# Third mixer's inverse in 32x32 and 64x64 blocks at its two last levels; end of the down projection by token groups

## The chip, the cores and the metric

The kernel runs on one core of a Trainium2 chip (trn2). The metric is the device time of one execution in microseconds (us), the median of several runs. The core has TensorE (matmuls, written PE in the profile; PEld are its weight loads), VectorE (DVE), ScalarE (ACT), GpSimd (POOL) and SyncE (SP, which issues transfers here).

## The reference, cut to what matters

One inference step of a decoder layer for 1072 tokens: 16 learned tokens, 1024 prompt tokens, and 8 sequences of 4 tokens. All is fp32.

```python
z = rms(x) @ w_in                         # 1024 -> 7704 columns: four mixers and gates
# mixer 1 HGRN2, mixer 2 RWKV-7, mixer 3 GLA, mixer 4 mLSTM, 4 heads each
# RWKV-7, per token and head (64 x 64 state S):
#   S = S * w_t - (S @ kk_t) outer (kk_t * a_t) + v_t outer k_t ;  y_t = S @ r_t
mix = sum(proj(o_n, w_branch[n]) * sigmoid(gate_n) for n in 4 mixers) @ w_out
x = x + mix
x = x + square(relu(rms(x) @ w_up)) @ w_down      # 1024 -> 4096 -> 1024
y = x * rsqrt(mean(x * x) + 1e-6) * norm_final
```

The RWKV recurrence is evaluated 128 tokens at a time. Within such a tile the tokens depend on each other through a strictly triangular 128 by 128 matrix per head, and the tile's outputs need the inverse of the unit triangular matrix made from it.

## The kernel before, in words

Tokens lie along the free dimension of the tiles, channels along the 128 partitions. The 1056 tokens that have an output (all but the 16 learned ones) are cut into three groups of 352 for every large matmul (`part2(g)`). The large products are made of three fp32r matmuls each: high part times high part, high times low, low times high. The high part is a rounding copy (ScalarE `ACT.Copy`, or VectorE), the low part the difference (`split_lo`, L602). The mixers run in the order mLSTM, then HGRN2 and GLA together, then RWKV-7, which is the third stage of mixer work and is called the third mixer here.

**The third mixer's tiles.** There are eight tiles of 128 tokens (`rw_tile`) and a last one of 48. A tile holds its four heads side by side. TensorE first makes the products of the tile: for each head three fp32 matmuls over the head's 64 channels (L1302 to L1304). Heads 0 and 2 lie on partitions 0 to 63, heads 1 and 3 on 64 to 127. VectorE masks them (L2437, L2458, L2463). Then the inverse is built by doubling: block size 1, 2, 4, 8, 16, 32, 64. At level `l`, with half-size `lh`, TensorE multiplies the off-diagonal matrix with half of the columns of the inverse so far (L1316), ScalarE copies the product to SBUF (L1765), TensorE multiplies from the other side (L1337, and L1331 for the transposed inverse at level 5), and VectorE puts the needed entries in place with a predicated copy (`select`, L2482). For levels 1 to 4 VectorE gets the transposed inverse by a stream transpose (L2447). All these matmuls use the full 128 by 128 matrices, though at the last levels only blocks of 32 by 32 or 64 by 64 are kept by the masks. An fp32 matmul is two records in the profile.

The order on each engine is written out by hand, and engines meet in semaphores. While TensorE would wait for ScalarE or VectorE it does steps of other work: `steps(gate, k)` issues k steps of the gates' input projection (`fill_work`; a step is the three matmuls of L463, 352 columns each). ScalarE takes each finished filler result out of PSUM (L498) between its own steps. On VectorE an increment of the semaphore `select_turn` stands before each predicated copy.

**The end.** The down projection runs in four passes `jj` of two output rows (a row is 128 channels) each: for each of the 32 rows `r` of the hidden layer, ScalarE makes the high part (L1864), VectorE the low part (L602) into two alternating buffers, and TensorE does, for both output rows `v`, the three groups and three products (L1464, 18 matmuls). Every fourth row VectorE also splits a chunk of weights (L598, L602). The passes are a hardware loop. In the last pass, ScalarE squares the first six rows of x (L568), and GpSimd adds the squares up (L575). After the pass, VectorE adds the residual for the rows 6 and 7 (L2672), they are squared and added one after the other, all 1056 tokens wide; TensorE sums over partitions with a matrix of ones (L561, fp32), ScalarE makes the scale with Ln and Exp (L589, L591), and the eight output rows are multiplied, five on VectorE (L2695) and three on GpSimd (L990; ScalarE has multiplied those by norm_final before). SyncE sends each row when it is done (L728), in 8 transfers.

## Time and profile before

| | us |
|---|---|
| median of 3 runs | 2201.63 (2198.26 to 2205.15) |
| profiled execution, its own time | 2207.53 |
| its span, first to last instruction | 2205.9 |
| TensorE busy | 2126.6 |
| VectorE busy | 1038.6 |
| ScalarE busy | 610.8 |
| GpSimd busy | 452.0 |

Times in the profile count from the start of the span. A busy TensorE isn't one at its peak: the ends of its matmuls are modelled and overlap, so how far apart matmuls start says more than their durations. The granted clock is given as a share: 1.00 is 2.4 GHz, 0.50 is 1.2 GHz.

### The profile page before, as it was taken

To read this page: it belongs to the slowest core of one execution; us is meant where nothing else is said; L and a number is where in the kernel's file an instruction comes from. 1 tells how busy PE (TensorE), PEld (TensorE's weight loads), DVE (VectorE), ACT (ScalarE), POOL (GpSimd) and SP (SyncE) were. 2 spreads that over 40 slices of the span, in tenths; PEclk is the share of its full clock that TensorE was granted. 3 is DMA by queue.
4 is the path that set the end of the run, shared out by engine and by line. 5 is a ranking of instruction groups with operands and counts; after the bars stand their busy time and mean duration, and the time that the engine had idled before them with its cause. 6 is when DMAs were issued, how large, how long until landed. Compare 5 with 4: busy or idle time off the path is not lost.

```text
span 2205.9 us, 32891 instructions
## 1 busy us (share of the span) xinstructions
PE 2126.6 (96%) x13203; PEld 2020.8 (92%) x13203; DVE 1038.6 (47%) x1538; ACT 610.8 (28%) x808; POOL 452.0 (20%) x463
## 2 busy tenths in 40 slices
PE   6999999999999989999999999999999999999995
PEld 4998889999999878989899999999999999999994
DVE  4052333566655454343443786522222245665654
ACT  4432224332323163221221541100000023333352
POOL 1122113343544411100001672200000010000022
PEclk9999999999999989999999999999999999999997
DMA  4122125221222322111012762221111251111112
GB/s 163 48 51 83 58 88 167 76 63 63 82 63 86 120 89 69 31 38 39 19 39 98 264 206 88 98 67 48 47 39 67 92 203 55 48 38 48 47 39 88
DMA packets 48705, 177.29 MB, mean 80 GB/s; under 512 B 6416, under 2 KB 6896, under 8 KB 48384
## 3 DMA queue, kind: packets, MB, share of 16 engines
q1 hardware_dynamic: 23184, 85.65, 12.4%
q0 software_dynamic: 17648, 61.31, 8.1%
q10 hardware_dynamic: 7808, 29.41, 3.6%
q8 instruction: 47, 0.77, 0.2%
q14 instruction: 18, 0.15, 0.0%
HBM read 128.84 MB, written 47.51 MB: 80 GB/s over the span
## 4 chain that ended last, share of the span: by engine, by line
PE 85%; DVE 6%; DMA 4%; issue 2%; ACT 2%; POOL 1%; DVEq 0%; SPq 0%; ACTq 0%; POOLq 0%
PE PS L463 27%; PE PS L624 21%; PE PS L1464 16%; PE PS L1337 2%; PE PS L1148 2%; PE PS L1316 2%; PE PS L1426 1%; DMA RING<-in_w_br 1%; PE PS L1160 1%; DVE AR L2135 1%; DMA AR<-proj 1%; PE PS L1009 1%; PE PS L1278 1%; PE PS L1286 1%; DVE CF_parts L598 1%
## 5 line engine op out<-in xcount | busy, mean ns | idle before, releaser
L463 PE MATMUL PS<-HT_parts,WHIA_parts 128*128 128x352 f32 (+1 forms) x1440 | 511.1, 355 | 11.4 <-ACT AR L498 4.1
L463 PE MATMUL PS<-OT_parts,WHIA_parts 128*128 128x352 f32 (+1 forms) x1440 | 474.9, 330 | 0.0
L463 PE MATMUL PS<-HT_parts,RING_parts 128*128 128x352 f32 (+1 forms) x1440 | 473.9, 329 | 0.0
L458 POOL TENSOR_TENSOR RING_parts<-RING,WHIA_parts 128x1024 fp32r<-128x1024 f32 x60 | 151.1, 2519 | 750.3 <-ACT WHIA_parts L453 750.3
L463 PEld LDWEIGHTS PS<-HT_parts,WHIA_parts 128*128 128x128 f32 x1440 | 277.6, 193 | 25.8 <-issue 12.7
L463 PEld LDWEIGHTS PS<-OT_parts,WHIA_parts 128*128 128x128 f32 x1440 | 277.3, 193 | 3.6
L463 PEld LDWEIGHTS PS<-HT_parts,RING_parts 128*128 128x128 f32 x1440 | 276.7, 192 | 0.0
L1464 PE MATMUL PS<-MIXHI_parts,CF_parts 128*128 128x352 f32 x768 | 250.5, 326 | 4.0 <-DVEq L2674 3.0
L624 PE MATMUL PS<-HT_parts,CF_parts 128*128 128x352 f32 x768 | 249.7, 325 | 0.9 <-ACT AR L591 0.9
L1464 PE MATMUL PS<-MIXHI_parts,RING_parts 128*128 128x352 f32 x768 | 249.6, 325 | 0.0
L624 PE MATMUL PS<-HT_parts,RING_parts 128*128 128x352 f32 x768 | 248.4, 323 | 0.0
L624 PE MATMUL PS<-OT_parts,CF_parts 128*128 128x352 f32 x768 | 248.4, 323 | 0.0
L1864 ACT ACTIVATE MIXHI_parts<-AR 128x1056 fp32r<-128x1056 f32 x96 | 104.3, 1087 | 170.1 <-PE PS L1464 164.5
L1464 PEld LDWEIGHTS PS<-MIXHI_parts,CF_parts 128*128 128x128 f32 x768 | 145.1, 189 | 5.9 <-DVEq L2674 3.8
L624 PEld LDWEIGHTS PS<-HT_parts,CF_parts 128*128 128x128 f32 x768 | 144.4, 188 | 1.3 <-ACT AR L591 1.2
L624 PEld LDWEIGHTS PS<-OT_parts,CF_parts 128*128 128x128 f32 x768 | 145.1, 189 | 0.1
L1464 PEld LDWEIGHTS PS<-MIXHI_parts,RING_parts 128*128 128x128 f32 x768 | 144.8, 188 | 0.0
L624 PEld LDWEIGHTS PS<-HT_parts,RING_parts 128*128 128x128 f32 x768 | 144.6, 188 | 0.0
L2634 DVE SCALAR_TENSOR_TENSOR AR<-PS,AR 128x1056 f32 (+1 forms) x32 | 40.2, 1258 | 199.9 <-PE PS L624 193.5
L1464 PE MATMUL PS<-LO_parts,CF_parts 128*128 128x352 f32 x384 | 124.8, 325 | 0.0
L1464 PE MATMUL PS<-CF_parts 128*128 128x352 f32 x384 | 124.6, 324 | 0.0
L575 POOL TENSOR_TENSOR AR<-AR 128x1056 f32<-128x1056 f32 x14 | 33.4, 2385 | 435.6 <-ACT AR L568 435.6
(399 smaller groups left out, 3533.0 us busy)
## 6 DMA issues: line engine op xcount, KB each, us to landing
RING<-in_w_all SPq DMA_DIRECT2D x132, 512.0 KB, 3.3
AR<-gates POOLq DMA_DIRECT2D x32, 528.0 KB, 4.0
proj<-AR ACTq DMA_DIRECT2D x18, 537.0 KB, 5.0
AR<-proj POOLq DMA_DIRECT2D x18, 537.0 KB, 7.3
gates<-CF ACTq DMA_DIRECT2D x16, 528.0 KB, 5.0
gates<-AR ACTq DMA_DIRECT2D x16, 528.0 KB, 5.4
AR<-in_xT SPq DMA_DIRECT2D x8, 537.0 KB, 8.6
AR<-in_xT POOLq DMA_DIRECT2D x8, 528.0 KB, 6.9
```

The costliest lines, as they stand in the source:

```text
L458: e.tensor_tensor(RING_R[:, u], RING[:, u], WHIA_R[:, u].bitcast(F32), ALU.subtract).then_inc(S(f"split{u}"), 1)
L463: last = e.matmul(out, a_[:, u, k, :], b_[:, k, t], start=first and i == 0, stop=end and i == 2)
L575: e.tensor_tensor(sq[:, 0, T2], sq[:, 0, T2], sq[:, 1, T2], ALU.add).then_inc(S("norm_sum"), 1)
L598: return e.tensor_copy(hi, x)
L624: last = e.matmul(PS(3 * u + g, 0, G2), a_[:, u, k, :], b_[:, k, t], start=k == 0 and i == 0, stop=k == KD - 1 and i == 2)
L1009: last = e.matmul(PS(3 + g, 0, GRP)[0:68], WS[:, k, :], XT[:, k, g * GRP:(g + 1) * GRP], start=k == 0, stop=k == KD - 1)
L1148: last = e.matmul(PS(3 * (l % 2), lo * m, hi * m)[0:w], x[:, g, l, 0:w], GQB[:, l % 2, lo * m:hi * m], start=True, stop=True)
L1316: last = e.matmul(PS(4, h * m, h * m + m)[0:w], pb[0:w, 2 * h * w:2 * h * w + w], side, start=True, stop=True)
L1337: last = e.matmul(PS(0, h * m, h * m + m)[0:w], a_[0:w, h * w:h * w + w], b_, start=True, stop=True)
L1464: last = e.matmul(PS(3 * v + g, 0, G2), a_[:, u, 4 * v + r % 4, :], b_[b][:, t], start=r == 0 and i == 0, stop=r == 31 and i == 2)
L1864: e.activation(AHI_R[r % 2][:, T2], act_row(r)[:, T2], ACT.Copy).then_inc(S("act_hi"), 1)
L2634: e.scalar_tensor_tensor(row2(dst), cols2(3 * u), 0.0, row2(RST2), ALU.max, ALU.mult).then_inc(S(f"banks_free{u}"), 1)
```

## The change

Part 1, third mixer, on TensorE alone. The products at a tile's start are issued so that the two partition halves alternate (all nine tiles). At levels 5 and 6 (`lh` 32 and 64) of the eight full tiles, the matmuls are done for the kept blocks only: for each head, two blocks of 32 by 32, or one of 64 by 64, with 32 or 64 partitions contracted. The block lists hold 8 matmuls at level 5 and 4 at level 6, for each group. Two increments of `select_turn` are added on TensorE in each of these levels.

Part 2, the end. The last pass of the down projection is written out behind a loop of three. Its rows 28 to 31 get high and low buffers of their own, and their matmuls are ordered by token group: group 0 for both output rows, then group 1, then group 2. Residual, square, sum, scale and output of each group of 352 tokens follow on their engines, interleaved. GpSimd adds the squares by groups (for the last row of group 2, TensorE adds the square in a second matmul), VectorE makes all output rows, and SyncE sends pairs of rows by group, 12 transfers.

```diff
+        SQ4 = Arena(3 * W).take(t=W)
+        LAST_ROWS = 28
+        LAST_HI = {28: MIXHI_R[:, 0], 29: MIXHI_R[:, 2], 30: MIXHI_R[:, 4], 31: AHI_R[0]}
+        LAST_LO = {28: MIXHI_R[:, 1], 29: MIXHI_R[:, 3], 30: MIXHI_R[:, 5], 31: ALO_R[0]}
+        SUMS_OF_6 = KD - 1 + KD // 2 + 5
...
+        def group_sum_pe(e, g):
+            e.wait_ge(S("norm_sum"), SUMS_OF_6 + (2, 4, 5)[g])
+            if g == 2:
+                e.wait_ge(S("rstd"), 3)
+            last = e.matmul(PS(6 + g % 2, 0, G2), ones, SQ3[:, 0, part2(g)], start=True, stop=g < 2)
+            if g == 2:
+                e.wait_ge(S("norm_sq"), 2 * KD + 6 + 2 * (g + 1))
+                last = e.matmul(PS(6, 0, G2), ones, SQ4[:, part2(g)], start=False, stop=True)
+            last.then_inc(S("sq_used"), 1)
...  (SyncE)
+            for g in range(3):
+                for k in range(0, KD, 2):
+                    e.wait_ge(S("y_done"), g * KD + k + 2)
+                    e.dma_start(ys[k:k + 2, :, part2(g)].rearrange("k p t -> p k t"), HN2[:, k:k + 2, part2(g)]).then_inc(S("y_out"), 16)
...  (GpSimd)
+            for g in range(3):
+                for v, sq in enumerate((SQ3[:, 1], SQ4)[:1 if g == 2 else 2]):
+                    e.wait_ge(S("norm_sq"), 2 * KD + 6 + 2 * g + v + 1)
+                    e.wait_ge(S("norm_sum"), SUMS_OF_6 + 2 * g + v)
+                    total = SQ3[:, 0, part2(g)]
+                    e.tensor_tensor(total, total, sq[:, part2(g)], ALU.add).then_inc(S("norm_sum"), 1)
...  (TensorE, third mixer)
-                for h in range(4):
-                    r, g = slice(64 * (h % 2), 64 * (h % 2) + 64), h // 2
-                    ab = rc[r, g:g + 3:2, 0:w]
-                    e.matmul(PS(h % 2, ...), rc[r, 6 + g, 0:w], ab, ...)
-                    e.matmul(PS(2 + h % 2, ...), rc[r, 4 + g, 0:w], ab, ...)
-                    last = e.matmul(PS(4 + h % 2, ...), rc[r, g, 0:w], rc[r, 6 + g, 0:w], ...)
+                for g in range(2):
+                    for k in range(3):
+                        for b in range(2):
+                            r = slice(64 * b, 64 * b + 64)
+                            (the same matmul k for half b)
...
+                    firsts, seconds = ([slice(j, j + lh) for j in range(o, w, 2 * lh)] for o in (0, lh))
+                    small = not last_tile and lh >= 32
+                    blocks = [(h, j, f, s) for h in range(4) for j, (f, s) in enumerate(zip(firsts, seconds))] if small else []
+                    if small:
+                        e.sem_inc(S("select_turn"), 1)
+                    for h, j, f, s in blocks:
+                        last = e.matmul(PS(4, h * m + j * lh, h * m + j * lh + lh)[f], pb[s, 2 * h * w + f.start:2 * h * w + f.stop],
+                                        tt[s, h * w + s.start:h * w + s.stop], start=True, stop=True)
...
+                    if small:
+                        e.sem_inc(S("select_turn"), 1)
...
+                        for h, j, f, s in blocks:
+                            last = e.matmul(PS(1, h * m + j * lh, h * m + j * lh + lh)[s], m1[f, h * w + s.start:h * w + s.stop],
+                                            ti[f, h * w + f.start:h * w + f.stop], start=True, stop=True)
...
+                    for h, j, f, s in blocks:
+                        last = e.matmul(PS(0, h * m + j * lh, h * m + j * lh + lh)[f], ti[f, h * w + f.start:h * w + f.stop],
+                                        m1[f, h * w + s.start:h * w + s.stop], start=True, stop=True)
...  (TensorE, end)
+            with e.Fori(0, 3) as jj:
+                down_rows(jj, FF // P)
+            down_rows(3, LAST_ROWS)
+            e.wait_ge(S("split1"), 3 * 4 + P_DOWN + 4)
+            for g in range(3):
+                for v in range(2):
+                    for r in range(LAST_ROWS, FF // P):
+                        e.wait_ge(S("act_parts"), 3 * 32 + r + 1)
+                        last = down_row(3, r, v, g, LAST_HI[r], LAST_LO[r])
+                    last.then_inc(S(f"down{v}"), 1)
+                    if g and v == 0:
+                        group_sum_pe(e, g - 1)
+            group_sum_pe(e, 2)
...  (ScalarE)
+                    if last and r >= LAST_ROWS:
+                        e.wait_ge(S("act_used"), 3 * 32 + min(r - 2, 29))
+                        e.activation(LAST_HI[r][:, T2], act_row(r)[:, T2], ACT.Copy).then_inc(S("act_hi"), 1)
+                        continue
...
+            group_square(0, 0)
+            group_square(0, 1)
+            for g in range(1, 3):
+                group_square(g, 0)
+                group_rstd(g - 1)
+                group_square(g, 1)
+            group_rstd(2)
...  (VectorE)
+            group_residual(0, 0)
+            group_residual(0, 1)
+            for g in range(1, 3):
+                group_residual(g, 0)
+                outputs(g - 1, 0, 4)
+                group_residual(g, 1)
+                outputs(g - 1, 4, KD)
+            outputs(2, 0, KD)
```

`group_residual`, `group_square`, `group_rstd` and `outputs` are the former operations on 352 columns; each waits for the operation that feeds it.

## Rows read from the trace of the kernel before

**Rows 1.** The page: busy time by engine; the chain that ended last.
```profile
PE 2126.6 (96%) x13203; PEld 2020.8 (92%) x13203; DVE 1038.6 (47%) x1538; ACT 610.8 (28%) x808; POOL 452.0 (20%) x463
...
PE 85%; DVE 6%; DMA 4%; issue 2%; ACT 2%; POOL 1%; DVEq 0%; SPq 0%; ACTq 0%; POOLq 0%
```
**Rows 2.** Windows: stretch, length, busy time (count) by engine, granted clock, DMA.
```profile
980.00:1020.00 40.00, 39.53 (x294) 36.19 (x293) 18.21 (x45) 9.32 (x22) 2.35 (x1) 1.00 0.09 27
...
2140.00:2173.00 33.00, 33.00 (x205) 33.00 (x204) 17.33 (x15) 14.02 (x13) 0.00 (x0) 1.00 0.09 32
2173.00:2206.00 33.00, 5.86 (x19) 3.54 (x17) 14.59 (x7) 4.39 (x4) 12.56 (x5) 0.64 0.33 131
```
**Rows 3.** Timeline, TensorE, a tile's first products: start, duration, operation, [idle before].
```profile
935.75 0.70 PE L1302 MATMUL PS<-AR 64*128 64x256 f32 x2
936.29 0.38 PE L1303 MATMUL PS<-AR 64*128 64x256 f32 x1
936.29 0.48 PE L1302 MATMUL PS<-AR 64*128 64x256 f32 x1
...
938.66 0.43 PE L463 MATMUL PS<-HT_parts,WHIA_parts 128*128 128x352 f32 x1
```
**Rows 4.** Timeline, TensorE, levels 32 and 64 of the same stage.
```profile
955.73 0.97 PEld L1316 LDWEIGHTS PS<-AR 128*128 128x128 f32 x8
955.84 1.00 PE L1316 MATMUL PS<-AR 128*128 128x64 f32 x8
...
960.03 1.10 PE L1316 MATMUL PS<-AR 128*128 128x64 f32 x8
```
**Rows 5.** Timeline, TensorE, the last tile of 48 tokens.
```profile
1153.23 0.32 PE L463 MATMUL PS<-HT_parts,RING_parts 128*128 128x352 f32 x1
1153.48 0.43 PEld L1316 LDWEIGHTS PS<-AR 48*48 48x48 f32 x8 [0.22 <-issue]
...
1153.95 0.19 PEld L463 LDWEIGHTS PS<-HT_parts,WHIA_parts 128*128 128x128 f32 x1
```
**Rows 6.** Windows around 1192, groups of its first stretch, and timeline behind it.
```profile
1188.60:1192.00 3.40, 3.40 (x30) 3.18 (x30) 3.21 (x4) 0.50 (x2) 0.00 (x0) 1.00 0.02 5
1192.00:1195.40 3.40, 3.40 (x16) 3.18 (x15) 1.28 (x3) 0.18 (x1) 0.00 (x0) 0.51 0.00 0
...
L1375 PE MATMUL PS<-AR 48*128 48x128 f32 x14 | 2.8, 279 | 0.0
...
1195.86 0.49 PE L463 MATMUL PS<-HT_parts,WHIA_parts 128*128 128x352 f32 x1
1196.15 0.49 PE L463 MATMUL PS<-OT_parts,WHIA_parts 128*128 128x352 f32 x1
```
**Rows 7.** Chain that ended last, in order of time, behind the last large matmul.
```profile
2179.34 2.06 POOL AR L575
...
2181.54 3.87 PE PS L561 x6
...
2187.73 3.21 DVE OT L2695
...
2194.32 5.49 DVE OT L2695 x3
```
**Rows 8.** Groups by form; line L840; timeline of VectorE.
```profile
L498 ACT ACTIVATE AR<-PS 128x352 f32<-128x352 f32 x45 | 20.7, 459 | 109.0 <-PE PS L463 109.0
...
L840 POOL TENSOR_TENSOR AR<-AR,CF x60: 350/621/734, 404.6 to 721.7; 128x256 f32<-128x256 f32 x56, 128x96 f32<-128x96 f32 x4
...
934.00 0.61 DVE L2554 SCALAR_TENSOR_TENSOR AR<-AR 128x128 f32<-128x128 f32 x2
...
2161.64 1.25 DVE L602 TENSOR_TENSOR CF_parts<-HT,MIXHI_parts 128x1056 fp32r<-128x1056 f32 x1
```
**Rows 9.** Lines L2695 and L728: duration min/median/max in ns; landing.
```profile
L2695 DVE SCALAR_TENSOR_TENSOR OT<-OT,CC,AR x5: 1305/3105/3455, 2187.7 to 2198.5; 128x1056 f32<-128x1056 f32 x5
...
DMA to landing us min/median/max: 2.7/3.7/5.2
```

More of the change, by code:

```diff
@@ L420, in build @@
         SQ3R = Arena(2 * W).take(t=W)
-        Y3 = Arena(3 * W).take(k=3, t=W)
+        SQ4 = Arena(3 * W).take(t=W)
[3 more added lines that the diff above has]
+        SUMS_OF_6 = KD - 1 + KD // 2 + 5
         xs, ys = A["xT"], OUT["yT"]
@@ L1313, in rw_tile @@
                         e.wait_ge(S("rw_t"), t0 + (RW_LOWER if l == 1 else rw_tt(l - 1, False)))
-                    for h in range(4):
+                    firsts, seconds = ([slice(j, j + lh) for j in range(o, w, 2 * lh)] for o in (0, lh))
[6 more added lines that the diff above has]
+                                        tt[s, h * w + s.start:h * w + s.stop], start=True, stop=True)
+                    for h in range(0 if small else 4):
                         side = half(ti[0:w, h * w:h * w + w], lh, False) if last_tile else half(tt[0:w, h * w:h * w + w], lh, True)
@@ L1328, in rw_tile @@
                         last.then_inc(S("rw_n"), 1)
+                    if small:
+                        e.sem_inc(S("select_turn"), 1)
                     if not last_tile and RW_FLIPS < l < nlev - 1:
-                        for h in range(4):
-                            last = e.matmul(PS(1, h * m, h * m + m)[0:w], m1[0:w, h * w:h * w + w],
-                                            half(ti[0:w, h * w:h * w + w], lh, False), start=True, stop=True)
+                        for h, j, f, s in blocks:
+                            last = e.matmul(PS(1, h * m + j * lh, h * m + j * lh + lh)[s], m1[f, h * w + s.start:h * w + s.stop],
+                                            ti[f, h * w + f.start:h * w + f.stop], start=True, stop=True)
                         last.then_inc(S("rw_n"), 1)
-                    for h in range(4):
+                    for h, j, f, s in blocks:
+                        last = e.matmul(PS(0, h * m + j * lh, h * m + j * lh + lh)[f], ti[f, h * w + f.start:h * w + f.stop],
+                                        m1[f, h * w + s.start:h * w + s.stop], start=True, stop=True)
+                    for h in range(0 if small else 4):
                         a_, b_ = (m1, half(tt[0:w, h * w:h * w + w], lh, True)) if last_tile else \
@@ L1448, in _, with down_row, down_rows @@
                 pe_split_pair(e, i + P_UP, i + EV_UP, HT_R, OT_R)
-            with e.Fori(0, 4) as jj:
-                for r in range(FF // P):
-                    q, b = r // 4, r % 2
-                    u = q % 2
+            def down_row(jj, r, v, g, hi, lo):
+                u = r // 4 % 2
+                for i, (a_, b_) in enumerate(((WHI_R, hi), (WHI_R, lo), (RING_R, hi))):
+                    last = e.matmul(PS(3 * v + g, 0, G2), a_[:, u, 4 * v + r % 4, :], b_[:, part2(g)],
+                                    start=r == 0 and i == 0, stop=r == 31 and i == 2)
+                return last
+            def down_rows(jj, end):
+                for r in range(end):
                     if r % 4 == 0:
-                        e.wait_ge(S(f"split{u}"), jj * 4 + (P_DOWN + q // 2 + 1))
+                        e.wait_ge(S(f"split{r // 4 % 2}"), jj * 4 + (P_DOWN + r // 8 + 1))
                     e.wait_ge(S("act_parts"), jj * 32 + (r + 1))
@@ L1461, in _ @@
                         for g in range(3):
-                            t = part2(g)
-                            for i, (a_, b_) in enumerate(((WHI_R, AHI_R), (WHI_R, ALO_R), (RING_R, AHI_R))):
-                                last = e.matmul(PS(3 * v + g, 0, G2), a_[:, u, 4 * v + r % 4, :], b_[b][:, t],
-                                                start=r == 0 and i == 0, stop=r == 31 and i == 2)
+                            last = down_row(jj, r, v, g, AHI_R[r % 2], ALO_R[r % 2])
                         if r == 31:
@@ L2690, in _, with group_residual, outputs @@
             down_parts(3, False, True)
-            for v in range(2):
-                add_residual(6 + v, 3, v)
-            e.wait_ge(S("rstd"), 3)
-            for k in range(3, KD):
-                e.scalar_tensor_tensor(HN2[:, k, T2], HN2[:, k, T2], col("norm_final", k), SQ3R[:, T2],
-                                       ALU.mult, ALU.mult).then_inc(S("y_done"), 1)
+            def group_residual(g, v):
+                e.wait_ge(S(f"down{v}"), 3 + g + 1)
+                x = HN2[:, 6 + v, part2(g)]
+                e.tensor_tensor(x, PS(3 * v + g, 0, G2), x, ALU.add).then_inc(S("dn_ready"), 1)
+            def outputs(g, lo, hi):
+                e.wait_ge(S("rstd"), 3 + g)
+                e.wait_ge(S("dn_ready"), 6 + 2 * g + 2)
+                for k in range(lo, hi):
+                    y = HN2[:, k, part2(g)]
+                    e.scalar_tensor_tensor(y, y, col("norm_final", k), SQ3R[:, part2(g)], ALU.mult, ALU.mult).then_inc(S("y_done"), 1)
+            group_residual(0, 0)
[6 more added lines that the diff above has]
+            outputs(2, 0, KD)
 def kernel(**inputs):
```

53 lines of the change are left out of this document (21 added, 32 removed).

## The prediction

> **What bounds the kernel now.** I read the page first: TensorE is busy 96% of the span and carries 85% of the chain that ended last [rows 1], so time is won where TensorE has less to stream or where it isn't working. The windows tell the two kinds of stretch apart [rows 2]. In the third mixer's stage (980 to 1020) and in the down projection (2140 to 2173) TensorE is busy nearly all the time, at a granted clock of 1.00. In the last 33.0 us it does 5.9 us of work, and everything else there waits on a chain. The change works on both: it makes small matmuls of the third mixer smaller, eight tiles long, and it cuts the end into three token groups.
>
> The large matmuls (352 columns) start 0.161 us apart (33.00 us for 205) [rows 2]. One filler step is three of them, 0.48 us.
>
> **Part 1a: first products of a tile, order changed.** The reader sees twelve fp32 matmuls (two records each) with 64 rows, from 935.75 to the next filler at 938.66, 2.91 us [rows 3]. Head 0 uses rows 0 to 63, head 1 rows 64 to 127. Head 1's first record starts at 936.29, together with a record of head 0: the two row halves run side by side, but only once the first head's products are handed out, 0.54 us late. At the end the last head runs alone in the same way. With the halves alternating from the first matmul the 0.54 us goes. Ends: nothing (if the pair doesn't start together) and 0.54; a loss is excluded, as the same records run on the same halves. I take 0.47, for eight tiles 3.8 us.
>
> **Part 1b: levels 32 and 64 in blocks.** In level 32 (the fifth of six) TensorE issues three groups of four matmuls, in level 64 two. Each is 8 records, 128 by 128 weights and 64 columns. The weight loads of a group take 0.97 us with 0.19 for one, so they start (0.97-0.19)/7 = 0.111 apart, whatever the columns [rows 4]. From level 32's first group at 955.84 to level 64's at 960.03 the chain group, ScalarE copy, groups, VectorE select takes 4.19 us, of which 24 records are 2.67. The price of a smaller matmul is seen in the last tile: 48 by 48 weights load in 0.43 us for 8 with 0.12 for one, 0.044 apart [rows 5]. A line through 128 and 48 gives 0.057 for 64 and 0.031 for 32.
> - Level 64: 16 records stay 16: 16 x (0.111-0.057) = 0.87 us less a tile.
> - Level 32: 24 records become 48 (two blocks a head): 24 x 0.111 - 48 x 0.031 = 1.18 us less. Ends: 48 x 0.044, the 48-wide row itself, leaves 0.55; if the two blocks' row groups run side by side as the halves do in [rows 3], 48 x 0.016 gives 1.90. I take the line, since the small loads of the last tile share one row group and so show no such gain.
> - Added: changing between block shapes. Before the 48-wide group the gap from the last filler is 0.25 us instead of 0.16, and behind it about 0.05 more [rows 5]. Three of the five groups start after a wait in which TensorE is idle anyway, so entry is paid once or twice, exit four times: 0.27. Four semaphore increments in TensorE's queue per tile: 0.15, from nothing (in the wait's shadow) to 0.3. Behind them stand the blocks and the filler, and ScalarE and VectorE wait for the blocks.
> - Everything shortened is both TensorE time and the chain of the level; the filler, the ScalarE copy and the VectorE select stay as they are. So it comes off the tile.
> Sum: 0.87 + 1.18 - 0.42 = 1.63 us a tile, 13.0 us for eight. Ends: 0.2 a tile and 2.5 a tile.
>
> The Trainium skill (TensorEngine Tiling, Key Properties) says that changing the tiling mode drains TensorE while merely another tile doesn't. The row agrees in kind, and puts the gap at 0.09 us in and 0.05 out [rows 5]. By the rule alone, with a full drain at each of the five groups, the part would be worth what the second rival gives; by the row it keeps nearly all.
>
> **Part 1c: the clock.** This speaks against the change. From 1188.6 to 1192.0 TensorE is busy without a break, nearly all in matmuls that fill 48 of 128 rows (14 from L1375, and as many from its neighbour in the same loop); then the granted clock is 0.51, the lower level (1.2 of 2.4 GHz), and the large matmuls start 0.29 apart [rows 6]. There the clock fell behind a stretch of partly filled matmuls, though the engine was never idle. In levels 32 and 64 today all small matmuls fill 128 rows and the clock is 1.00. Afterwards they fill 32 or 64, and the filler is what remains. Four filler steps in about 5.5 us are left as full work; I take it that in about three of the eight tiles the clock falls for one stretch, costing two or three steps at +0.39 and some small ones, 1.5 us each: 4.5 us lost. Ends: 0 and 14 us (every tile, with its neighbour stretch).
>
> Stage sum: -3.8 - 13.0 + 4.5 = -12.3 us.
>
> **Part 2: the tail.** Now: TensorE's work behind 2173 is 5.86 us, 3.87 of it the sum [rows 2, 7], so the last large matmul ends near 2175.0; the end is 30.9 us later. In the chain: residual add, square, GpSimd add (2.05), square, GpSimd add, sum at the lower clock (3.87), two ScalarE passes of 1.1, outputs from 2187.7 to 2199.8 [rows 7], and the last write before the span's end at 2205.9.
>
> After, by groups. A 352-wide operation costs: PSUM copy on ScalarE 0.46, so 0.5 for square, Ln or Exp [rows 8]; GpSimd add 0.77 (between 0.62 for 256 and 2.05 for 1056) [rows 7, 8]; output on VectorE 0.5 (two 128-wide in 0.61 with 0.35 each, so 0.26 apart; 1.305 for 1056) [rows 8, 9]; residual add 0.5. Walking it on the clock of the trace:
> - Rows 28 to 31 of the hidden layer must have their low parts before the first group is through. ScalarE gets ahead (separate buffers), but VectorE makes row 28's from 2161.64 [rows 8] and each takes 1.2, so the fourth is done at 2166.5. TensorE is there from 2163.1, and wants it 1.4 us later. It finishes the first (group, half) at 2167.1 instead of 2165.1: a new stall of 2.0 us.
> - Five more of 12 matmuls (1.93 each), with two group sums between (0.6 each). Group 0: residuals at 2167.4 and 2169.3, second square at 2170.4, GpSimd at 2171.2, sum until 2172.2, Ln and Exp until 2173.4.
> - From 2173.5 VectorE is the bound: 24 outputs of 0.5 (12.0), three residual adds (1.5), GpSimd's adds in between. The row of before shows what those do: outputs on VectorE take 3.1 to 3.5 us while GpSimd adds, 1.3 alone [rows 9]; I put each overlapped add at its own 0.7 us, twice. Group 1's scale waits for the residual that VectorE's queue holds behind four outputs, then square, GpSimd, sum, Ln and Exp: 1.6 us idle. For group 2, 1.0 (its sum probably at the lower clock). Together 17.5, so 2191.0.
> - The last write lands 3.7 us after its issue [rows 9], plus 0.3: 2195.0. The early groups' writes are out by then, so no queue of 528 KB writes stands ahead.
> Saved: 2205.9 - 2195.0 = 10.9, I take 11. Ends: 6 (GpSimd's adds overlap fully, TensorE's clock falls during the stall) and 16 (no stall, no overlap). TensorE finishes later than now, around 2180; it isn't what ends last. The copies for the first three output rows that go from ScalarE were under the down projection: nothing. Writing the fourth pass out rather than looping: nothing, up to 2 us if the code comes late.
>
> **Sum.** -12.3 - 11 = -23.3 us against the profiled execution's 2207.53 (span 2205.9). That run lies 5.9 us above the median of three, 2201.63, so I subtract from the median: 2178 us. Its own range, from the ends of the terms with most of them not at their worst together: 2166 to 2192.
>
> **Rivals.**
> 1. The clock takes back part 1. For it: [rows 6]. Against: filler remains between all groups, and the stage stands at 1.00 throughout. Every tile loses 1.7 us: -16.8 + 14 - 11 = -14, 2188 us.
> 2. Drains and increments cost as much as the blocks save. For it: the gap in [rows 5]. Against: that gap is only 0.14 in all. A group would pay 0.3 us: the levels then gain 0.2 a tile, and -3.8 - 1.6 - 11 = -16, 2185 us.
> 3. The tail's saving goes into VectorE's queue (outputs ahead of residual adds, each in turn behind GpSimd) and only 3 us are left: 2186 us. For it: VectorE's 15 us of work stand where there were 12. Against: they start 14 us sooner.
> 4. Slower: the clock falls in level 32 and stays down until the next tile's full-row matmuls. The place is the filler: some 14 steps between 955.8 and 970, each +0.39 us. The gains without clock are 27.8 us, so it decides from 71 steps, nine a tile; with 14 in each of eight tiles it costs 44 us, 2218 us. For it: a clock once lost at 1192.0 is still down in full-row filler at 1195.9 [rows 6]. Against: it needs every tile.
> 5. The changed parts aren't on the path: nothing moves. Against: both stand in the chain.
>
> **Chances.** Forecast 0.70; rival 1 0.12; rival 2 0.06; rival 3 0.04; rival 4 0.05; rival 5 0.03. Differences under 0.3% (6.6 us) can't be told from no change. The first four are faster, less 0.01 for those that shrink below the bound: faster 0.91, within 0.04, slower 0.05. The range of all cases with a tenth outside at each end: 2165 to 2194.
>
> **What would show it.** L1302's group 0.5 us shorter with both halves from the start; level 64's matmuls about 0.057 apart, level 32's 0.03; windows of the stage at a clock below 1.00 if part 1c holds; a TensorE stall of 2 us at row 28; VectorE the last engine, with outputs of 0.5 us each, and the end some 15 us after TensorE's last large matmul. Wrong it is if level 32's records stand 0.045 or more apart, if dips are found in most tiles, or if the last write is later than 2199 on the old clock with the stage's saving taken off.

## The result and the profile after

The changed kernel takes 2162.05 us (median of 4 runs, 2161.61 to 2164.84), the kernel before beside it 2200.74 (2198.26 to 2205.15): 38.7 us less, ratio 0.982, 95% interval 0.980 to 0.984. A later series gave 2164.38 (6 runs) beside 2205.47 (11 runs), ratio 0.982 (0.979 to 0.985). I had forecast 2178.0 with a range of 2165 to 2194. The sign and the two places were right; the gain is 1.6 to 1.7 times the forecast one (38.7 against 23.3 to 23.6), and the first median lies 3 us below the range.

The page of the changed kernel, the two lines that answer to [rows 1]: TensorE has 29.5 us less to do, and the share of the other engines in the chain falls.
```profile
PE 2097.1 (97%) x13397; PEld 1988.9 (92%) x13397; DVE 1038.8 (48%) x1561; ACT 609.0 (28%) x813; POOL 448.9 (21%) x463
...
PE 87%; DVE 5%; DMA 2%; ACT 2%; issue 2%; POOL 0%; DVEq 0%; SPq 0%; ACTq 0%; POOLq 0%
```
Windows of the changed kernel (columns as in [rows 2]): a whole tile of the third mixer, level 32, level 64, and everything behind the last large matmul.
```profile
1023.10:1055.60 32.50, 32.11 (x282) 28.86 (x280) 14.50 (x37) 8.02 (x18) 2.38 (x1) 1.00 0.11 33
...
945.17:947.63 2.46, 2.38 (x56) 1.79 (x55) 0.45 (x1) 0.66 (x2) 0.70 (x1) 1.00 0.00 0
947.63:950.10 2.47, 2.47 (x23) 2.10 (x24) 0.82 (x2) 0.38 (x1) 0.00 (x0) 1.00 0.00 0
...
2147.50:2159.90 12.40, 2.05 (x7) 0.68 (x5) 8.55 (x17) 1.91 (x4) 0.28 (x1) 0.74 0.67 243
```
Level 32 was 4.19 us long [rows 4] and is 2.46; level 64 went from 3.14 (960.03 to 963.17, where the next group of full matmuls starts in the timeline of before) to 2.47. The granted clock is 1.00 in the three windows of the stage. From one tile's first product to the next one's it was 35.41 us and is 32.58, six tiles in a row. What follows the last large matmul took 31 us and takes 12.4.

The weight loads of a group of small matmuls, timeline of the changed kernel; they answer to [rows 4].
```profile
945.17 0.33 PEld L1339 LDWEIGHTS PS<-AR 32*32 32x32 f32 x16
...
947.60 0.54 PEld L1339 LDWEIGHTS PS<-AR 64*64 64x64 f32 x8 [0.34 <-issue]
```
A single one of these loads takes 0.11 and 0.13 us. So 32 by 32 blocks start (0.33-0.11)/15 = 0.015 us apart, and 64 by 64 blocks (0.54-0.13)/7 = 0.059. The prediction had 0.031 and 0.057.

TensorE at a tile's first products (answers to [rows 3]): from 925.52 to the filler at 927.89 are 2.37 us; it was 2.91.
```profile
925.52 1.14 PE L1319 MATMUL PS<-AR 64*128 64x256 f32 x8
...
927.57 0.39 PE L1322 MATMUL PS<-AR 64*128 64x128 f32 x4
927.89 0.43 PE L467 MATMUL PS<-HT_parts,WHIA_parts 128*128 128x352 f32 x1
```

The tail, timeline of TensorE and then of VectorE in the changed kernel, and at the end the landing of the twelve output writes (L741).
```profile
2130.84 0.49 PE L1486 MATMUL PS<-MIXHI_parts,CF_parts 128*128 128x352 f32 x2
...
2131.83 0.59 PE L1486 MATMUL PS<-MIXHI_parts,CF_parts 128*128 128x352 f32 x2 [0.34 <-DVE MIXHI_parts L617]
...
2133.00 0.59 PE L1486 MATMUL PS<-MIXHI_parts,CF_parts 128*128 128x352 f32 x2 [0.42 <-DVE MIXHI_parts L617]
...
2134.16 0.43 PE L1486 MATMUL PS<-MIXHI_parts,CF_parts 128*128 128x352 f32 x1 [0.41 <-DVE CF_parts L617]
...
2134.76 0.48 PE L1486 MATMUL PS<-MIXHI_parts,CF_parts 128*128 128x352 f32 x2
```
```profile
2134.96 0.53 DVE L2751 TENSOR_TENSOR OT<-PS,OT 128x352 f32<-128x352 f32 x1 [0.85 <-PE PS L1486]
...
2140.89 2.07 DVE L2758 SCALAR_TENSOR_TENSOR OT<-OT,CC,AR 128x352 f32<-128x352 f32 x4 [1.54 <-ACT AR L606]
...
2153.00 4.06 DVE L2758 SCALAR_TENSOR_TENSOR OT<-OT,CC,AR 128x352 f32<-128x352 f32 x8 [0.62 <-ACT AR L606]
```
```profile
DMA to landing us min/median/max: 2.4/2.4/2.5
```
The first twelve matmuls of rows 28 to 31 run from 2130.84 to 2134.76, 3.92 us for 12 x 0.161 = 1.93: the stall is 2.0 us, and each of its three parts ends when VectorE has made a low part (L617). VectorE is then the last engine, to 2157.06.

Stretches in which the granted clock is at its lower level (half-clock stretches) lie in other places from profile to profile. To compare profiles all the same, I cut each at the same instructions (first product of each tile, first matmul of the up projection, first matmul of the down projection, end):

| profile | to the first tile | eight tiles | one tile, median | last tile to up projection | down projection to end |
|---|---|---|---|---|---|
| before | 865.9 | 282.4 | 35.41 | 177.2 | 411.3 |
| changed | 859.5 | 261.5 | 32.58 | 171.9 | 397.8 |

The stage and the tail give 20.9 + 13.5 = 34.4 of 46.0 us between these two profiled executions. The other 11.6, 6.4 ahead of the stage and 5.2 behind it, lie in code that the change doesn't touch, but for the last tile's products. The clock goes with them: ahead of the first tile it stood at 0.50 for 47.8 us before and for 37.5 in the changed kernel, between the last tile and the up projection for 6.8 and for nothing.

### The profile page after: what moved, and what is told of

It is laid out like the page before. It is cut to its first block, busy times and chain, and to the rows that moved or that the text cites. A ratio compares the mean times of both kernels' runs of the same rounds, so it can differ in the third digit from the quotient of the medians.

```text
span 2159.9 us, 33312 instructions
## 1 busy us (share of the span) xinstructions
PE 2097.1 (97%) x13397; PEld 1988.9 (92%) x13397; DVE 1038.8 (48%) x1561; ACT 609.0 (28%) x813; POOL 448.9 (21%) x463
## 4 chain that ended last, share of the span: by engine, by line
PE 87%; DVE 5%; DMA 2%; ACT 2%; issue 2%; POOL 0%; DVEq 0%; SPq 0%; ACTq 0%; POOLq 0%
PE PS L467 29%; PE PS L639 22%; PE PS L1486 16%; PE PS L1458 2%; PE PS L1164 2%; PE PS L1369 2%; PE PS L1343 2%; DMA RING<-in_w_all 1%; PE PS L1176 1%; DMA RING<-in_w_br 1%; PE PS L1319 1%; PE PS L1025 1%; PE PS L1294 1%; PE PS L1302 1%; DVE CF_parts L613 1%
## 5 line engine op out<-in xcount | busy, mean ns | idle before, releaser
L462 POOL TENSOR_TENSOR RING_parts<-RING,WHIA_parts 128x1024 fp32r<-128x1024 f32 x60 | 156.7, 2612 | 725.5 <-ACT WHIA_parts L457 725.4
L467 PEld LDWEIGHTS PS<-HT_parts,WHIA_parts 128*128 128x128 f32 x1440 | 275.5, 191 | 25.0 <-issue 12.3
L2689 DVE SCALAR_TENSOR_TENSOR AR<-PS,AR 128x1056 f32 (+1 forms) x32 | 40.2, 1258 | 199.7 <-PE PS L639 193.3
L590 POOL TENSOR_TENSOR AR<-AR 128x1056 f32<-128x1056 f32 x12 | 29.4, 2446 | 394.1 <-ACT AR L583 394.1
```

Of the source, the lines that this page charges most:

```text
L462: e.tensor_tensor(RING_R[:, u], RING[:, u], WHIA_R[:, u].bitcast(F32), ALU.subtract).then_inc(S(f"split{u}"), 1)
L467: last = e.matmul(out, a_[:, u, k, :], b_[:, k, t], start=first and i == 0, stop=end and i == 2)
L590: e.tensor_tensor(sq[:, 0, T2], sq[:, 0, T2], sq[:, 1, T2], ALU.add).then_inc(S("norm_sum"), 1)
L2689: e.scalar_tensor_tensor(row2(dst), cols2(3 * u), 0.0, row2(RST2), ALU.max, ALU.mult).then_inc(S(f"banks_free{u}"), 1)
```

## Experiments

**The parts one by one, and the order of the blocks.** The first three are the kernel before with one part of the diff: `e1_products` the order of the first products, `e2_blocks` the blocks of levels 32 and 64, `e3_tail` the tail. The fourth is the changed kernel with
```
-blocks = [... for h in range(4) for j, (f, s) in enumerate(...)]
+blocks = [... for j, (f, s) in enumerate(...) for h in range(4)]
```


> The kernel before with one edit: the twelve first products of a tile in the new order (both row halves in turn from the first matmul). Theory: the three parts of the change are independent, and this one takes 0.5 us off each of eight tiles (2.91 us from the first product to the next filler in the trace of before, 2.37 in that of the changed kernel): 4.3 us, so 2196.5 us beside 2200.7. The same stretch shows 2.37 us in this kernel's trace. Rival: 1.0 us a tile between two tile starts belongs to the new order (what the levels don't account for), as the next step comes sooner too: 8 us, 2193. Where the half-clock stretches lie may differ from the kernel before in code that nobody changed.

> The kernel before with one edit: levels 32 and 64 of the third mixer's inverse in 32x32 and 64x64 blocks. Theory: 1.73 us (level 32) and 0.67 us (level 64) come off each of eight tiles, as in the trace of the changed kernel: 19 us, 2181.5 beside 2200.7; level 32 takes 2.46 us instead of 4.19. My prediction had 13 us here and 4.5 us lost to the clock: by it 2192. Rival, the clock helps: the half-clock stretches of the mixers behind this stage go away because of the blocks, which gives about 5 us more, 2176.

> The kernel before with one edit: the last pass of the down projection, norm and output by token groups. Theory: it takes 13.5 us off, as the two profiles show from the last pass to the end (27.1 of 31.2+... us counted from the offset ahead of the down projection): 2187.2 beside 2200.7. Prediction: 11, so 2189.7. In this kernel's trace the third mixer's tiles are 34.9 us apart as before, and everything up to the last pass is as before except where half-clock stretches fall.

> The changed kernel with the order of level 32's small matmuls turned: all heads' first blocks (one row group), then all heads' second blocks (another row group), instead of the two in turn. Theory: blocks on different row groups run side by side (records 0.0167 us apart in the changed kernel), and on one row group they stand 0.031 to 0.044 apart: 16 records take 0.6 to 0.85 us instead of 0.44, 0.7 to 1.3 us a tile, so 5.5 to 10.5 us slower: 2168 to 2173 beside 2162. Rival: a 32x32 block costs 0.017 us wherever it lies (the time goes with its columns), and the order changes nothing: 2162.

Measured, beside 2203.53 of the kernel before (18 runs):

| kernel | us | ratio, 95% | one tile | eight tiles | last tile to up projection | down projection to end |
|---|---|---|---|---|---|---|
| products alone | 2199.01 | 0.996 to 1.000 | 34.88 | 279.9 | 173.3 | 411.2 |
| blocks alone | 2186.78 | 0.990 to 0.994 | 33.11 | 265.7 | 178.2 | 411.4 |
| tail alone | 2192.43 | 0.992 to 0.996 | 35.39 | 283.9 | 175.0 | 397.9 |
| changed, blocks by row group | 2165.11 | 0.982 to 0.987 | 32.98 | 263.1 | 171.6 | 397.9 |

- Per tile the parts add up: 35.41 - 34.88 = 0.53 and 35.41 - 33.11 = 2.30, together 2.83, and 35.41 - 32.58 is 2.83. The rival of the products (1.0 us a tile) is out: in their kernel the twelve take 2.37 us as in the changed one. The blocks are worth 8 x 2.30 = 18.4 us, not 13.0.
- The tail's 13.4 us stand alone too. In every profile that has the tail as in the changed kernel, the down projection to the end takes 397.8 to 398.5 us, in those without it 411.2 to 411.4.
- The medians give 4.5, 16.8 and 11.1, together 32.4; whole and sum differ by 6 to 9 us, about what the intervals of the three (4 to 5 us to each side) allow.
- Row groups (a row group is the 32 partitions that a block contracts over): the same 16 loads, of the kernel with the blocks in order of row group:
```profile
944.90 0.48 PEld L1339 LDWEIGHTS PS<-AR 32*32 32x32 f32 x16
```
(0.48-0.11)/15 = 0.025 us apart, against 0.015 when two row groups take turns. Over 48 records that is 0.48 us, and the tile is 0.40 longer, 3.2 us in eight. The theory's mechanism is there, at a third to a little over half of its price (5.5 to 10.5 us): on one row group a 32-wide load starts after 0.025 us, not 0.031 or 0.044. One rival is left: a head's two blocks differ in the 32 partitions that their result lands on (`PS(...)[f]`) as well as in those they contract over, and this order turns both at once. So what is shown is blocks of two places in turn against blocks of one place; that it is the row group alone isn't. The medians are no further apart than 1 to 3 us, too little to tell by them alone.

**What holds the clock up.** The changed kernel with the other four levels in 32 by 32 matmuls as well (`e5_all_levels`):
```
+diag = [(h, b, slice(32 * b, 32 * b + 32)) for h in range(4) for b in range(4)]
+for h, b, d in diag:
+    last = e.matmul(PS(4, h * m + 16 * b, ...)[d], pb[d, ...], half(tt[d, ...], lh, True), ...)
```
and the changed kernel with the filler of levels 32 and 64 moved (`e6_filler_moved`):
```
-steps(gate, 6 if last_tile else 1)
+steps(gate, 6 if last_tile else 0 if small else 1)
...
-steps(gate, 3 if last_tile else 6)
+steps(gate, 3 if last_tile else 10)
```


> The changed kernel, and the four levels below 32 in the same manner: each of their two groups of four 128x128 matmuls (8 records, 64 columns) becomes sixteen 32x32 matmuls on the diagonal (32 records, 16 columns), four row groups in turn. Theory: the records are handed out 0.017 us apart or closer, so a group takes 32 x 0.017 = 0.53 us instead of 8 x 0.111 = 0.89: 0.36 less, 0.14 of it lost again where the shape of block changes, for eight groups in each of eight tiles 14 us off: 2148 beside 2162, with a clock of 1.00 in the stage. Rival, my prediction's term for the clock: with no small matmul of 128 rows left in the inverse the granted clock falls in some tiles, at 3 to 5 us each, and the gain is lost: 2162 or above, with half-clock stretches between 860 and 1120. Second rival: 32 records have a price of their own of over 0.028 us and nothing is gained.

> The changed kernel, with the four filler steps of levels 32 and 64 (twelve large matmuls) moved behind the levels, to the end of the tile. It asks what keeps the clock up. If the filler does, as my prediction had it, the granted clock falls between 860 and 1120 in most tiles, and the time is the exposed waits (four steps of 0.48 us a tile, 15 us in all) and some 1.5 to 5 us a tile more: 2190 to 2215. Theory now: the clock stands at 1.00 as the stage's other work is enough, and only the exposed waits count: 2175 to 2178.

Beside 2202.73 of before, all levels gave 2157.07 (ratio 0.976 to 0.980) and the moved filler 2204.37 (1.000 to 1.003). Windows of the kernel with all levels: the second tile up to where its clock falls, the stretch behind that, and the third tile.
```profile
892.90:906.30 13.40, 12.56 (x288) 10.26 (x286) 8.29 (x20) 3.67 (x7) 0.00 (x0) 1.00 0.28 82
906.30:926.80 20.50, 20.49 (x175) 18.18 (x161) 2.79 (x6) 3.10 (x7) 7.08 (x6) 0.50 0.10 27
931.20:960.50 29.30, 28.40 (x474) 24.65 (x472) 14.78 (x38) 8.06 (x18) 2.36 (x1) 1.00 0.13 39
```
Where the clock stays up for a whole tile it takes 29.4 to 31.1 us, with a median of 29.6, 3.0 less than in the changed kernel: more than the 1.8 expected. In two of eight tiles the clock falls for 20.5 us, and they take 38.3 and 39.0. Price and threat were both real, and nearly cancel: the eight tiles together take 258.4 us, 3.1 less than in the changed kernel. The timeline shows why the price was better; 32 records on four row groups in turn (16 columns each, where those of level 32 have 32) start (0.34-0.11)/31 = 0.007 us apart, in other groups 0.008:
```profile
935.79 0.34 PEld L1343 LDWEIGHTS PS<-AR 32*32 32x32 f32 x32 [0.22 <-issue]
```
Windows of the kernel with the filler moved: the fall in one tile, and a stretch as long as a tile that holds a fall.
```profile
994.10:1000.90 6.80, 6.80 (x32) 6.80 (x32) 0.11 (x1) 0.38 (x1) 0.00 (x0) 0.50 0.00 0
...
1080.10:1118.30 38.20, 35.80 (x287) 33.11 (x287) 14.67 (x36) 8.13 (x18) 2.36 (x1) 0.91 0.09 28
```
The clock falls in every one of the eight tiles, for 6.8 to 10.2 us, and stays down in full-row filler as in [rows 6]. A tile takes 36.5 to 38.2 us. So it is the filler between the groups that keeps the clock up in the changed kernel; my theory of that moment (2175 to 2178) was wrong, and the prediction's reason for a small price was right. The edit does two things at once, though: large matmuls are missing there, and TensorE idles 2.1 to 2.4 us in each tile where it idled 0.3 to 0.5.

**Two rows instead of four in the tail's groups** (`e8_two_rows`: `LAST_ROWS = 30`).

> The changed kernel, with two last rows of the hidden layer by token groups instead of four. The stall of TensorE in the last pass (rows 28 to 31 want low parts that VectorE has not made) goes: its last large matmul ends 2 to 3 us sooner on the down projection's own clock. But the first group's sum of products is there only four half-groups from the end of 1.0 us each, instead of 1.9, so group 0's residuals come at nearly the same time or up to 1.2 us later. Theory: VectorE's queue of outputs and adds sets the end, so the time follows group 0: between 1.2 us slower and the same, 2162 to 2163.5. Rival: TensorE's end sets the last group's sum and output, and 2 us are won: 2160.

2164.76 (0.981 to 0.985), and 400.4 us from the down projection to the end, 2.7 more than the changed kernel. The first residual add starts 375.7 us behind the down projection's first matmul, where it was 372.8; that is the timeline's
```profile
2137.40 0.53 DVE L2751 TENSOR_TENSOR OT<-PS,OT 128x352 f32<-128x352 f32 x1 [2.12 <-PE PS L1486]
```
On that clock the first output comes 2.0 us later and the last eight 2.7 later; the 0.7 between is TensorE's last sum, two matmuls that took 1.54 us at the lower clock instead of 0.86. The stall is gone and nothing is won by it: what counts here is when group 0 is through. The forecast loss of up to 1.2 us was too small in the profile (the medians, 0.4 to 2.7 us above those of the changed kernel, can't tell), and TensorE's last large matmul came 2.5 us later, not sooner, since the groups' sums stand ahead of it in TensorE's queue and wait for GpSimd.

**Which small matmuls, and whose idle time.** `e9_levels_2_4` and `e10_levels_8_16` turn only those levels into 32 by 32 matmuls; `e11_before_filler_moved` is the kernel before with the edit of the filler shown above, where the small matmuls are 128 by 128; the fourth is the changed kernel again.

> The changed kernel, and only the two lowest of the other levels (2 and 4) in 32x32 matmuls on the diagonal; levels 8 and 16 keep their 128x128 matmuls. With all four levels so, a tile took 29.6 us instead of 32.58 where the clock stayed, but the granted clock fell for 20.5 us in two of eight tiles. Theory: half of the gain, 1.48 us a tile, and the clock holds, as four groups of full matmuls are left: 12 us off, 2150. Rival: the clock falls again in some tiles (9 us for each stretch of that kind), and it is 2160 or above.

> The changed kernel, and levels 8 and 16 in 32x32 matmuls on the diagonal; levels 2 and 4 keep their 128x128 matmuls. Theory: as with levels 2 and 4, 1.48 us a tile and no fall: 2150. Rival: here the small matmuls of levels 8 to 64 stand in one unbroken row of some 12 us, so if the clock answers to a whole stretch of small matmuls it falls here and not with levels 2 and 4: 2160 or above, with half-clock stretches in the stage.

> The kernel before with the four filler steps of levels 32 and 64 moved to the end of the tile, as was done to the changed kernel (where TensorE idled 2.35 us a tile, the clock fell in every tile and 42 us were lost). Here the small matmuls of these levels are 128 by 128. If full rows keep the clock up, as my prediction had it, the clock stays at 1.00 and only the exposed waits count, some 2 us a tile: 2203 + 16 = 2219. If the idle time alone brings the clock down, it falls in every tile here too: 2203 + 40 = 2243.

> The changed kernel once more, with more rounds, since the three parts alone came to 4.5, 16.8 and 11.1 us, 32 together, and the whole to 39 to 41. Theory: the rest is half-clock stretches in the mixers behind the stage (1168 to 1200), of which products alone had 3.4 us, blocks alone 10.2, the tail alone 6.8, and the whole none: this run shows none there again, 171.9 us from the last tile's start to the first matmul of the up projection, and 2162. Rival: the whole was timed in luck, with few runs, and more runs give 2165 to 2170.

| kernel | us | ratio, 95% | one tile | clock falls in the eight tiles |
|---|---|---|---|---|
| levels 2 and 4 | 2159.10 | 0.975 to 0.983 | 31.37 | none |
| levels 8 and 16 | 2161.38 | 0.976 to 0.984 | 31.05 | one, 3.4 us, in the first |
| before, filler moved | 2251.10 | 1.016 to 1.024 | 41.3 | every tile, 6.8 to 13.7 us |
| changed again | 2164.38 | 0.979 to 0.985 | 32.58 | one, 3.4 us, in the first |

(The one in the first tile, which begins at 860 to 868, is in the profile of the changed kernel as well.) Windows of the kernel before with its filler moved: a fall, and a stretch as long as a tile.
```profile
1096.30:1106.50 10.20, 9.65 (x45) 9.47 (x45) 0.62 (x2) 0.77 (x2) 0.00 (x0) 0.51 0.00 0
1071.00:1112.40 41.40, 39.33 (x258) 36.72 (x257) 14.58 (x36) 8.13 (x18) 2.36 (x1) 0.88 0.08 26
```
This is the run that decides on the prediction's part 1c. The small matmuls there fill all 128 rows, and the clock falls all the same, for 7 to 14 us (7 to 10 with the blocks). Full rows are not what protected the stage; the filler in between is, by its large matmuls or by the waits that it fills (TensorE idles 1.9 to 2.1 us a tile here, too). Yet the full small matmuls are not without effect: with the filler in its old places the clock held while levels 2 to 16 were made of them, and fell in two tiles when all four levels were small blocks. Two of the lower levels at a time cost no clock and bring 1.2 and 1.5 us a tile; the medians show less of it (1 to 5 us instead of the 12 forecast), and in both profiles the first tile starts at 867.8 to 869.8 instead of 859 to 864, in code that is the same. The changed kernel again shows 172.1 us behind the stage, and its median lies between theory and rival.

**What was still open.** `e12_last_tile_old` has the old order of products in the last tile alone. `e13_all_more_filler` is all levels in small matmuls with three filler steps moved from the tile's end between them:
```
-steps(gate, 6 if last_tile else 1)
+steps(gate, 6 if last_tile else 2 if l in (2, 3, 4) else 1)
...
-steps(gate, 3 if last_tile else 6)
+steps(gate, 3)
```
`e14_levels_4_8_16` leaves level 2 in full matmuls and the filler where it was.

> The changed kernel with the old order of the first products in the last tile (48 rows) alone. All five kernels with the old order show half-clock stretches of 6.8 us or more some 40 us behind the last tile's start, in a loop of matmuls that fill 48 of 128 rows, and take 175.0 to 178.2 us from that start to the up projection; eight of nine with the new order show none or one of 3.4 us and take 171.6 to 173.5. Theory: the 0.2 us by which the last tile's products are shorter shift that loop against the clock's fall, so with the old order back it takes 175 or more, and the time is 2167. Rival: which of them falls is luck of the run and of the eight tiles' sum, so 171.9 to 173.5 here, and 2163.

> All levels below 64 in 32x32 matmuls, with three of the six filler steps of the tile's end moved into levels 4, 8 and 16. Without that move a tile took 29.6 us where the clock stayed up, and two of eight tiles 8.6 to 9.3 us more (the clock fell 13.4 and 14 us into a tile). Theory: more full matmuls among the small ones keep the clock up in all eight tiles: 29.6 to 30 us a tile, 2162 - 8 x 2.8 = 2140 to 2143. Rival: TensorE idles at the tile's end instead, where the filler is now missing, and the clock falls there: 2155 or above.

> Levels 4 to 64 in small blocks, level 2 with its full 128x128 matmuls, filler where it was. Levels 2 and 4 so took 1.2 us off a tile, levels 8 and 16 1.55, both with no fall of the clock in the stage. Theory: 1.55 + 0.6 = 2.15 us a tile, 30.4 us, and the clock holds or falls in one tile: 2145 to 2155. Rival: it falls in two or more tiles as with all levels: 2157 or above.

Beside 2202.18 of before: 2159.17 (0.978 to 0.984) with the last tile's old order, 2140.82 (0.969 to 0.974) with more filler, 2178.72 (0.985 to 0.992) with level 2 full. The last is 24 us above the upper end of its theory, though in the profile the clock fell in one tile only, as the theory allowed: that tile took 40.2 us, the others 30.8 in the median instead of 30.4, and behind the stage 184.0 us passed, 20.5 of them at the lower clock. Windows of the kernel with more filler: one tile, all eight tiles.
```profile
954.00:983.60 29.60, 27.59 (x468) 23.97 (x464) 15.06 (x38) 8.19 (x19) 2.36 (x1) 1.00 0.12 39
...
865.90:1102.70 236.80, 227.14 (x3775) 198.23 (x3775) 114.51 (x280) 63.69 (x143) 23.62 (x13) 1.00 0.12 40
```
and the last of the eight tiles of the kernel with level 2 full, and its half-clock stretch:
```profile
1084.30:1124.50 40.20, 38.50 (x425) 34.18 (x424) 14.43 (x36) 7.38 (x18) 2.36 (x1) 0.75 0.09 28
```
```profile
1100.40:1120.90 20.50, 20.44 (x147) 18.66 (x148) 2.86 (x6) 1.47 (x5) 2.36 (x1) 0.50 0.01 2
```
With more filler among the levels all eight tiles keep a clock of 1.00, though TensorE idles 9.66 us in them (2.01 in the tile shown, where the tile that fell, with all levels small and the filler in its old places, idled 0.84 ahead of its fall and next to nothing behind it). So the idle time of a tile, by its sum, isn't what brings the clock down. The kernel with all levels says so by itself, in a tile that idled 2.22 us, more than the two in which the clock fell, and kept its clock:
```profile
1030.50:1061.60 31.10, 28.88 (x475) 24.84 (x474) 14.58 (x36) 8.52 (x19) 2.36 (x1) 1.00 0.12 36
```
Nor does idle time sort the runs over a shorter stretch: in the 6.1 us ahead of each fall, the kernel before with its filler moved idled 0.55 to 1.58 us; the kernel with more filler idled up to 1.42 us in a stretch of that length and kept its clock. What differs is how many large matmuls stand among the small ones of levels 4 to 16. That they hold the clock up fits this run and the two with moved filler; no run changed their number alone, with the waits as they were. The kernel with more filler is the fastest of all: 61 us below the kernel before, 21 to 24 below the changed one.

The stretch behind the stage, windows of the kernel with the blocks alone and then of the one with the last tile's old order:
```profile
1168.00:1182.00 14.00, 14.00 (x67) 13.06 (x67) 8.00 (x15) 0.97 (x3) 0.60 (x2) 0.63 0.00 1
```
```profile
1119.60:1291.59 171.99, 168.30 (x1140) 162.60 (x1139) 111.82 (x108) 61.77 (x72) 86.93 (x72) 1.00 0.56 189
```
The last tile's old order brings nothing back: 172.0 us from its start to the up projection, without a half-clock stretch. The theory of that run is refuted.

## Why the prediction missed by 15 us

The forecast gain was 23.3 us and the measured one 38.7. By the profiles, 5.4 of the missing 15.4 lie in part 1b (18.4 instead of 13.0), 4.5 in part 1c (a loss that didn't come), 2.5 in the tail and 0.4 in part 1a. The last 2.6 lie outside the changed code, where the prediction had no term. So two steps failed: the size of a 32 by 32 block in 1b, and the reason for a loss of clock in 1c.

- **Part 1a, 3.8 us:** right, 8 x 0.53 = 4.2. Both halves start together as in [rows 3].
- **Part 1b, 13.0 us: this is the step that failed most, in the size of a 32 by 32 block.** It took "the line", 0.031 us between records, where 0.015 was measured (its own lower end, "side by side", was 0.016). It gave as its reason that the small loads of the last tile show no such gain; but those loads all lie on the same partitions, and the new blocks don't. Of the 0.67 us a tile that are missing, 0.40 come from the two places in turn, as the fourth run shows, and 48 x (0.031-0.025) = 0.29 would be that one row group alone is quicker than the line through 128 and 48; the two overshoot by 0.02. I had seen the halves run side by side in [rows 3] and used it for the products alone. The 64-wide blocks are as the line had them (0.059 for 0.057). For the changes of shape and increments 0.42 was charged; with the measured level 32 the terms are 0.87 + 48 records' 1.94 - 2.40 = 0.41 by the lengths of the two levels (1.73 and 0.67 shorter), and 0.51 by the 2.30 that the tile gained. What the increments alone cost is not known: no run without them gave a time. The Trainium skill (TensorEngine Tiling (Array Packing), Key Properties) says both things, that tiles can load and multiply in parallel and that a change of mode drains the engine; I had weighed only the second, and the 0.015 in turn agrees with the first. The Trainium skill (TensorEngine Tiling (Array Packing), Performance Considerations) gives some 60 cycles of overhead to each matmul, which makes an estimate of 25 ns at 2.4 GHz; the measured 0.025 on one row group agrees with that, the 0.015 and 0.007 in turn don't.
- **Part 1c, 4.5 us lost: the other step that failed.** The loss didn't come: the eight tiles stand at 1.00 but for 3.4 us in the first. The reason given, that full 128-row matmuls had protected the stage, was wrong (the kernel before with its filler moved); the counter-reason, that filler remains, was right (the changed kernel with its filler moved). Nothing lost was one end of this term's range.
- **Stage:** 12.3 forecast, 8 x 2.83 = 22.6 measured between tiles at full clock.
- **Part 2, 11 us:** 13.5. Counted on the clock of before (the down projections start 32.5 us apart) the walk holds to a tenth for its first half (forecast in brackets): stall 2.0 us (2.0), residuals at 2167.4 and 2169.4 (2167.4, 2169.3), first output at 2173.4 (2173.5). VectorE's part took 16.2 us instead of 17.5: GpSimd's adds held up an output by half a microsecond at most. The line of the outputs, duration min/median/max in ns:
```profile
L2758 DVE SCALAR_TENSOR_TENSOR OT<-OT,CC,AR x24: 573/580/1126, 2140.9 to 2156.5; 128x352 f32<-128x352 f32 x24
```
  The writes landed 2.4 to 2.5 us after their issue, not 3.7; they are of two rows of 352 columns instead of one of 1056, and which of the two does it no run shows; the end is at 2192.4 instead of 2195.0.
- **The rest:** 36 us are accounted for by stage and tail. In the profiles of before and after 5.2 more are gone behind the stage and 6.4 ahead of it. Behind the stage, in one profile of each kernel (two of the changed one), the kernels with the old products and filler unchanged or moved (before, blocks alone, tail alone, before with filler moved) show 175.0 to 178.2 us with half-clock stretches of 6.8 or 10.2 us together; the changed kernel, twice, and its close kin (blocks by row group, two rows, last tile's old order) show 171.6 to 172.3 and none. Products alone, levels 2 and 4, levels 8 and 16 and the changed kernel with its filler moved stand between, at 173.3 to 173.5, and all levels, more filler and level 2 full have 177 to 184 again. So it seems to depend on the kernel and favours the changed one by 3 to 7 us, but what sets it is open: the last tile's products don't. Ahead of the stage the same code takes 858 to 870 us in sixteen profiles, and this goes with the clock: the seven that take 858 to 862 us have 31 to 41 us at 0.50 in it, the nine that take 864 to 870 have 44 to 51. What decides between them nothing that I tried explains.

Rivals: the clock that takes part 1 back, drains and the VectorE queue didn't come. The slower one, a clock that falls and stays down over the filler, came as soon as the filler was moved, with either form of the levels, and in single tiles when the inverse was nearly all small matmuls (all levels; level 2 full). Its 0.39 us a step (0.48 becomes 0.87) was a fair price: it makes 20.5 x 0.39 / 0.87 = 9.2 us of a stretch of 20.5, and the two tiles lost 8.7 and 9.4 against the median of 29.6.

## What to carry to other kernels

- Small matmuls of 32 or 64 rows should be issued so that neighbours lie on different row groups; here that took 32 by 32 blocks from 0.025 to 0.015 us apart with two groups, and blocks of half as many columns stood 0.007 apart with four. The result's partitions changed along with the row group in each case. If one pair of instructions in a trace already runs side by side, price every new pair of the same kind by it.
- Where the clock is at risk, look at what stands between the small matmuls. Three filler steps moved to another place in the same tile, nothing added or left out, decided between 2157 and 2141 us, and four of them moved out of levels 32 and 64 cost 40 to 46.
- A stall on an engine that isn't the last (2.0 us here) can be the cheap side of a trade: in the profile the version without it was 2.7 us slower from the down projection to the end, 0.7 of it by a lower clock.

## What the runs showed of the hardware

- Matmuls that fill all 128 rows, 64 columns each, don't keep the granted clock up by themselves: with the large matmuls taken from between those of two levels, and TensorE idle for 2 us a tile, it fell in eight of eight tiles.
- Conversely eight tiles with the inverse in 32 by 32 and 64 by 64 blocks and filler between them, with TensorE idle for 9.7 of 236.8 us, stayed at 1.00.
- Half-clock stretches fall in different places of identical code from kernel to kernel; ahead of the stage they sum to 31 to 51 us, and the same code takes 858 to 870. A difference between two single profiles should be cut at common instructions before any of it is put down to the change.
